# Last expert round taken out of the loop and added on TensorE, expert weights loaded in halves

## The reference, cut to what matters

```python
act = silu(xt @ exp_w1[e]) * (xt @ exp_w3[e]) * comb      # w1, w3: 1024 x 256 per expert
out = out + act @ exp_w2[e]                               # w2: 256 x 1024 per expert
y = rms_norm(x + out, final_norm_g)
```

## Time and profile before

| | |
|---|---|
| median of 3 runs | 716.58 us (715.87 to 720.83) |
| profiled execution, own time | 718.26 us |
| its span, first to last instruction | 716.3 us |
| mean granted TensorE clock | 0.931 |
| busy: TensorE, VectorE, ScalarE, POOL | 618.3, 319.0, 201.5, 79.2 us |
| moved by DMA | 179.38 MB, mean 250 GB/s |

### The profile page before, as it was taken

One profiled execution on the slowest core, in us unless ns is written; L12 is line 12 of the kernel. 1 busy time (PEld: TensorE's weight loads), 2 busy tenths in 40 slices (PEclk: granted clock), 3 DMA queues, 4 the chain that ended last, 5 costly groups with the idle time before them and its releaser, 6 DMA issues.

```text
span 716.3 us, 11504 instructions
## 1 busy us (share of the span) xinstructions
PE 618.3 (86%) x4673; PEld 451.2 (63%) x4673; DVE 319.0 (45%) x629; ACT 201.5 (28%) x343; POOL 79.2 (11%) x129
## 2 busy tenths in 40 slices
PE   4999999989899999999989985999999798398720
PEld 3999998579899999984778862333333343033200
DVE  4748978958544364688413155121121121012038
ACT  5512332254743434436003051121121121012022
POOL 0000000510001210010202111111212111110100
PEclk8999999999999999999989985999999999699965
DMA  9941220324556233669896394899999999999453
GB/s 284 279 141 64 96 82 2 121 79 125 168 129 214 81 118 119 234 239 342 277 389 254 150 350 181 337 420 420 418 421 421 418 422 419 422 420 402 190 233 136
DMA packets 74924, 179.38 MB, mean 250 GB/s; under 512 B 9166, under 2 KB 55946, under 8 KB 61544
## 3 DMA queue, kind: packets, MB, share of 16 engines
q1 hardware_dynamic: 65900, 163.47, 60.9%
q0 software_dynamic: 5600, 12.76, 4.7%
q10 hardware_dynamic: 3372, 2.42, 1.0%
HBM read 172.80 MB, written 15.61 MB: 263 GB/s over the span
## 4 chain that ended last, share of the span: by engine, by line
PE 68%; DMA 17%; DVE 6%; SPq 4%; issue 3%; ACT 2%; ACTq 1%; DVEq 0%; POOLq 0%
DMA w<-exp_w 13%; PE ps L1678 12%; PE ps L1680 12%; PE ps L1679 12%; PE ps L2121 11%; PE ps L2149 4%; PE ps L1827 3%; SPq L612 3%; PE ps L1674 3%; PE ps L1908 2%; DMA raw<-cache_mem_k 2%; DMA xs_rows<-x_sample 1%; PE ps L2008 1%; PE ps L1845 1%; PE ps L1970 1%
## 5 line engine op out<-in xcount | busy, mean ns | idle before, releaser
L2121 PE MATMUL ps<-w,xeT 128*64 128x512 f32 (+2 forms) x512 | 122.9, 652 | 22.9 <-DMA w<-exp_w 21.6
L1678 PE MATMUL ps<-xH,w_h 128*128 128x260 f32 x480 | 139.0, 290 | 0.4 <-DVE xL L1336 0.2
L1679 PE MATMUL ps<-xH,w_l 128*128 128x260 f32 x480 | 136.2, 284 | 0.0
L1680 PE MATMUL ps<-xL,w_h 128*128 128x260 f32 x480 | 136.2, 284 | 0.0
L2121 PEld LDWEIGHTS ps<-w,xeT 128*64 128x64 f32 (+2 forms) x512 | 42.2, 147 | 102.0 <-issue 100.2
L1678 PEld LDWEIGHTS ps<-xH,w_h 128*128 128x128 f32 x480 | 91.1, 190 | 5.6 <-issue 4.9
L1679 PEld LDWEIGHTS ps<-xH,w_l 128*128 128x128 f32 x480 | 91.0, 190 | 0.2
L1680 PEld LDWEIGHTS ps<-xL,w_h 128*128 128x128 f32 x480 | 91.1, 190 | 0.0
L1028 DVE TENSOR_TENSOR w_l<-raw,w_h 128x2048 fp32r<-128x2048 f32 x28 | 64.1, 2289 | 35.5 <-ACT w_h L725 35.5
L2149 PE MATMUL ps<-w,aT 128*64 128x512 f32 (+2 forms) x256 | 58.6, 598 | 9.3 <-DVE aT L1591 9.3
L1584 DVE SCALAR_TENSOR_TENSOR gated<-ps,rs_slot,silu 128x256 f32<-128x256 f32 x14 | 6.8, 483 | 122.3 <-ACT silu L966 122.3
(11 more groups left out here) (364 smaller groups left out, 920.2 us busy)
## 6 DMA issues: line engine op xcount, KB each, us to landing
w<-exp_w SPq DMA_DIRECT2D x96, 1024.0 KB, 21.7
raw<-w_in SPq DMA_DIRECT2D x8, 1024.0 KB, 11.1
raw<-cache_mem_k SPq DMA_DIRECT2D x8, 1024.0 KB, 6.8
raw<-cache_mem_v SPq DMA_DIRECT2D x8, 1024.0 KB, 12.1
raw<-xa_wk SPq DMA_DIRECT2D x4, 1024.0 KB, 5.9
raw<-xa_wv SPq DMA_DIRECT2D x4, 1024.0 KB, 5.7
raw<-xa_wq SPq DMA_DIRECT2D x4, 1024.0 KB, 5.1
raw<-xa_wo SPq DMA_DIRECT2D x4, 1024.0 KB, 5.2
```

Source lines behind the costliest of these rows:

```text
L1678: pe.matmul(out, h1, h2, start=start, stop=False)
L1679: pe.matmul(out, l1, h2, start=False, stop=False)
L1680: return pe.matmul(out, h1, l2, start=False, stop=stop)
L2121: last = pe.matmul(mm[0][half, j, :], xeT[j][:, k, half], w13[s][:, :, k, :], start=k == 0, stop=k == KT_D - 1)
```

## The change

It has these parts, all in one diff:

1. The last round (places 28 and 29, slots 2 and 3) stands behind the loop, and a turn of the loop is one round (places 30 and 31, slots 0 and 1, then those over capacity). The number of rounds is the same as before where the loop makes one turn. The gathers of the two are exchanged, so that the parity fits. The last round's transposes stand before the loop; the loop's turn ends with the transposes of a further gather, which is used only if there is another turn.
2. The last round's rows are not stored to `y_rows`. Instead TensorE adds them: per tile of tokens `x2` times the identity plus `ye[1]` times `back`, a 128 x 128 matrix that has the token's weight where row and token meet. VectorE's two adds come before it. ScalarE's squares and VectorE's last product read the sum from PSUM.
3. `back` is made in the routing, before `route_done`: the weights of the last round's rows by ten products of one column (`last_w`), and five fills.
4. Rows of `y_rows` that nobody stores to must be zero: VectorE fills `sumsq`, and SP writes it over `y_rows` by two transfers, after the eighth load of w_in.
5. `x2` is loaded by tiles, in the order of `TAIL`; `yr_in` counts both.
6. The gate and up weights are loaded in two halves of the contraction (4 KB per partition), with semaphores of their own; `hidden` waits for each half before its products, and counts `half_ready` after the fourth step, on which the next load of the first half waits.
7. Nine semaphores of the routing become two that count.

```diff
+TURNS = 1 + OVER // 2
+HALF = KT_D // 2 * FF
+TAIL = (0, 4, 1, 2, 3)
...
+        def in_whole(n_t):
+            return ps[(0, 2, 3, 1, 0)[n_t]][:].rearrange("p b d -> p (b d)")
...  (SP)
                 if c == 9:
+                    sp.wait_ge(zero_made, 1)
+                    zeros = sumsq[:, 0:SEQ].rearrange("p (o d) -> p o d", o=1)
+                    sp.dma_start(y_rows[0:8 * P].rearrange("(p a) (h d) -> p (a h) d", p=P, h=2),
+                                 zeros.broadcast_to([P, 16, SEQ])).then_inc(y_zeroed, 16)
+                    sp.dma_start(y_rows[8 * P:2 * T]...).then_inc(y_zeroed, 16)
...
+            def load_half(s, e, h):
+                dst = w13[s][:].rearrange("p w k f -> p w (k f)")
+                c = slice(h * HALF, h * HALF + HALF)
+                for n, src in enumerate((w1, w3)):
+                    sp.dma_start(dst[:, n:n + 1, c],
+                                 src[bass.ds(e, 1)].rearrange("o p f -> p o f")[:, :, c]).then_inc(w13_in[h][s], 16)
...
-                    sp.wait_ge(hid_ready, q + 1)
-                    for p, e in zip(coming, which):
-                        load_gate_up(p % RING, e)
+                    for h, free in enumerate((half_ready, hid_ready)):
+                        sp.wait_ge(free, q + 1)
+                        for p, e in zip(coming, which):
+                            load_half(p % RING, e, h)
...
             with sp.Fori(0, loops_n) as it:
-                for r in range(2):
-                    ...
+                which = [expert_at(it * 2 + (FIXED + 2 + n)) for n in range(2)]
+                ...
+            which = [expert_at(FIXED + n) for n in range(2)]
+            for h, free in enumerate((half_ready, hid_ready)):
+                sp.wait_ge(free, FREE_AT[1])
+                for n in range(2):
+                    load_half(2 + n, which[n], h)
+            sp.wait_ge(y_done, FREE_AT[1])
+            for n in range(2):
+                load_down(2 + n, which[n])
             sp.wait_ge(y_done, PAIRS)
-            sp.dma_start(x2[:, 0:4, :], x_rows[0:SEQ].rearrange("(t p) d -> p t d", p=P)).then_inc(x_back, 16)
-            sp.dma_start(x2[0:NS, 4, :], x_rows[SEQ:T]).then_inc(x_back, 16)
+            for t in TAIL:
+                t0, n = TILES[t]
+                sp.dma_start(x2[0:n, t, :], x_rows[t0:t0 + n]).then_inc(yr_in[t], 16)
...
-            for j in range(2):
-                wait(y_stored[j], loops_n * 16 + 16 * (PAIRS // 2))
+            wait(y_stored[0], loops_n * 16 + 16 * (PAIRS // 2))
+            sp.wait_ge(y_stored[1], 16 * (PAIRS // 2))
...  (ScalarE, before, in and after the loop)
+            columns_left(PAIRS + 1, 1)
             with act.Fori(0, loops_n) as it:
                 act.wait_ge(rs_made, it + 1)
+                silu_of(it + PAIRS, 0, rs_now[:, 0:1])
+                y_left(it + PAIRS, 0, it * 16 + 16 * (PAIRS // 2))
+                act.wait_ge(hid_ready, it + (PAIRS + 1))
+                columns_left(it + (PAIRS + 2), 0, False)
+            silu_of(loops_n + PAIRS, 1, rs_slot[:, PAIRS:PAIRS + 1])
+            y_left(loops_n + PAIRS, 1, 16 * (PAIRS // 2))
...  (VectorE, routing)
-            for i in range(1, OVER // 4):
+            for i in range(1, OVER // 2):
...
+            dve.scalar_tensor_tensor(last_hot[:], slot_f[:, 1], float(PAIRS), wgt[:], ALU.is_equal, ALU.mult).then_inc(last_hot_ready, 1)
+            link(dve.tensor_copy(row_f[:], gids[:, PAIRS:PAIRS + 1]))
+            dve.tensor_scalar(row_t[:], tile_no[:], row_f[:, 0:1], -1.0, ALU.subtract, ALU.mult)
+            src = take("last_w")
+            dve.tensor_copy(w_slot[:], src[:, 0:1]).then_inc(tv_used, 1)
+            dve.wait_ge(tv_used, TV_AT["last_w"] + 1)
+            for t in range(NT):
+                last = dve.tensor_scalar(back[:, t, :], count_to[:], row_t[:, t:t + 1], w_slot[:, 0:1], ALU.is_equal, ALU.mult)
+            last.then_inc(route_done, 1)
...  (VectorE, tail)
+            for n_t in range(2):
+                add_experts(TAIL[n_t])
+            dve.wait_ge(fg_in, 16)
+            for n_t in range(NT):
+                if n_t + 2 < NT:
+                    add_experts(TAIL[n_t + 2])
+                mean_square(n_t)
...  (TensorE, routing, behind rs_ids and before the first gathered_columns)
+            out = open_tv("last_w")
+            pe.wait_ge(last_hot_ready, 1)
+            for i in range(2):
+                for j, (_, n) in enumerate(TILES):
+                    last = pe.matmul(out[:, 0:1], row_hot[0:n, i, j, :], last_hot[0:n, i, j:j + 1], start=(i, j) == (0, 0),
+                                     stop=(i, j) == (1, NT - 1))
+            last.then_inc(tv_ready, 1)
...  (TensorE, hidden)
                 for k in range(KT_D):
+                    if k % (KT_D // 2) == 0:
+                        for s, count in loads:
+                            pe.wait_ge(w13_in[2 * k // KT_D][s], count * 32)
...
+                    if k == KT_D // 2 - 1:
+                        last.then_inc(half_ready, 1)
...  (TensorE, loop and behind it)
+            gathered_columns(PAIRS + 1, 1, PAIRS // 2 + 1)
             with pe.Fori(0, loops_n) as it:
+                ...
+                hidden(it + PAIRS, 0, slots, False)
+                act_columns(it + PAIRS)
+                down(it + PAIRS, slots)
+                gathered_columns(it + (PAIRS + 2), 0, it + (PAIRS // 2 + 2))
+            pe.wait_ge(xa_ready, loops_n + (PAIRS + 2))
+            pe.wait_ge(xv_ready, loops_n + (PAIRS + 2))
+            hidden(loops_n + PAIRS, 1, slots, False)
+            act_columns(loops_n + PAIRS)
+            down(loops_n + PAIRS, slots)
+            pe.wait_ge(ya_ready, loops_n + (PAIRS + 1))
+            pe.wait_ge(yv_ready, loops_n + (PAIRS + 1))
+            for n_t, t in enumerate(TAIL):
+                n = TILES[t][1]
+                pe.wait_ge(y_sum, n_t + 1)
+                if n_t == 4:
+                    pe.wait_ge(y_out, 1)
+                for b in range(2):
+                    c = slice(512 * b, 512 * b + 512)
+                    out = in_whole(n_t)[0:n, c]
+                    pe.matmul(out, ident[0:n, 0:n], x2[0:n, t, c], start=True, stop=False)
+                    last = pe.matmul(out, back[:, t, 0:n], ye[1][:, c], start=False, stop=True)
+                last.then_inc(whole, 1)
...  (POOL, loop)
+                wait(xt_done, it + (PAIRS + 2))
+                gather(0, g_idx[:, 0:1])
+                wait(y_stored[0], it * 16 + 16 * (PAIRS // 2))
+                ...
+                scatter(None, 0, s_idx[:, 0:1])
```

More of the change, by code:

```diff
@@ L65 @@
 OVER = 2 * T // CAP
-MORE_ITEMS = EXPERTS - FIXED + OVER
-COLS = PAIRS + MORE_ITEMS // 2 + 2
+TURNS = 1 + OVER // 2
+COLS = PAIRS + 2 + TURNS
 LIST = BAND
 assert COLS <= LIST
+HALF = KT_D // 2 * FF
 RING = 7
-TURNS = MORE_ITEMS // 4
+ROUTE_BY_PE = {"count": 1, "rank": 2, "block": 3, "starts": 4, "place": 5}
+ROUTE_BY_DVE = {"less": 1, "at_place": 2, "at_rank": 3, "over": 4}
 EXPERT_BYTES = 3 * SLOT_BYTES
@@ L461, in trunk_kernel @@
         out_stored = sem("out_stored")
-        w13_in = [sem(f"w13_in{i}") for i in range(RING)]
+        w13_in = [[sem(f"w13_in{i}_{h}") for i in range(RING)] for h in range(2)]
         w2_in = [sem(f"w2_in{i}") for i in range(RING)]
@@ L484, in trunk_kernel @@
         y_sum = sem("y_sum")
+        zero_made = sem("zero_made")
+        y_zeroed = sem("y_zeroed")
+        last_hot_ready = sem("last_hot_ready")
+        whole = sem("whole")
         y_sq = sem("y_sq")
@@ L487, in trunk_kernel @@
         y_root = sem("y_root")
-        y_out = [sem(f"y_out{i}") for i in range(NT)]
+        y_out = sem("y_out")
         y_saved = sem("y_saved")
         fg_in = sem("fg_in")
-        x_back = sem("x_back")
         route_done = sem("route_done")
@@ new lines, in _ @@
+                rounds = sp.value_load(free_at[0:1, bass.ds(it, 1)], min_val=1, max_val=PAIRS + TURNS)
+                for h, free in enumerate((half_ready, hid_ready)):
+                    wait(free, rounds)
+                    for n in range(2):
+                        load_half(n, which[n], h)
+                wait(y_done, rounds)
+                for n in range(2):
+                    load_down(n, which[n])
+            which = [expert_at(FIXED + n) for n in range(2)]
+            for h, free in enumerate((half_ready, hid_ready)):
+                sp.wait_ge(free, FREE_AT[1])
+                for n in range(2):
+                    load_half(2 + n, which[n], h)
```

216 lines of the change are left out of this document (96 added, 120 removed).

## The result

The changed kernel takes **723.91 us** (median of 7 runs, 722.2 to 726.01), the kernel before 717.62 beside it (7 runs, 714.93 to 720.83). The ratio is **1.0088, 95% interval 1.0068 to 1.0109**: certainly slower, by 6.3 us, just under what the prediction called 1% (7.2 us). The forecast was 716.9 with a range up to 722.

What follows compares the result with a forecast made beforehand. The expert part was taken as bound by an unbroken transfer queue from 458 us. Routing +7.7, early release -3.4, halves +0.5 made it 4.8 late; expert rows at 687.9 plus tail gave 716.65, adjusted to 716.9 us (range 708 to 722).

Steps and rivals of the forecast that it cites:

- The routing step: End of routing: new steps, including ten one-column calls at 4.3 us, start ScalarE's xeT of round 0 7.7 us late.
- The release of the first refill: Queue restart after round 0: halves release it 3.4 us earlier, so with routing 4.3 us later than before.
- The zeroing and VectorE's fill: Early, before TensorE's projections: expected free under cover; without it up to 10 us for zeroing and 0.64 for the fill.
- The tail from the first add: From 687.9 to 716.65 us: adds, sums, norm and store, with TensorE's first 5 us at the lower clock.
- the rival in which it stays low: Tail: TensorE stays at the lower clock, five tiles of 6.9 us, giving 730.6 us; chance 0.1.
- The last rounds: Rounds 14 and 15 on TensorE: start 656.4, last product ends 684.5, copies done 685.2 us.
- Halves, in the queue: Gate and up loads as 512 KB with 4 KB rows: 0.5 us taken from 0 to 3.7, queue 4.8 late.
- 4 KB rows pay 9 ns: Rival in the weight queue: a fixed cost per row adds 3.2 us, giving 720.1 us; chance 0.1.
- The early restart: Rival: queue restarts early, at -0.8 us lateness, giving 711.3 us, or 708.5 with the clock up; chance 0.17.
- the read-back ahead of the queue: Rival: expert rows are read without waiting behind the queue, tail starts at 685.2, giving 714.2 us; chance 0.15.
- a second turn: Rival: the loop makes two turns, adding 9.3 + 3.65 us and its transfers, about 730 us; chance 0.01.
- A fixed part of 0.22 for each transfer: Rival in the queue: a tenth of 2.2 us shows for each of 50 more transfers, 11 us, 727.9; chance 0.02.

Runs made afterwards that it cites:

- f_rows4k: Kernel before, each 1 MB gate and up load issued as two of 512 KB with 4 KB rows, released and awaited together; 724.26 us, ratio 1.0103.
- a_whole: Changed kernel with gate and up weights loaded whole again (1 MB, 8 KB rows); 723.70 us, ratio 1.0087.
- d_free_w: Changed kernel with the last round's weight column riding in the list of norm factors and the five fills after the first copies; 717.39 us, ratio 1.0004.
- e_waits: Changed kernel with TensorE's waits for ScalarE's copied columns moved behind products that don't read them; 726.90 us, ratio 1.0112.
- p_free_waits: Changed kernel, weight column in factor list, whole loads except halved first refill, copy waits behind products not needing them; 713.33 us, ratio 0.9933.
- j_both: Changed kernel with both the edits of d_free_w and e_waits, halves kept; 717.77 us, ratio 0.9995.
- c_mixed: Changed kernel with the upper half of the contraction loaded and multiplied first in every second slot; 728.57 us, ratio 1.0139.
- o_free_first: d_free_w with whole weight loads except the first refill, which is in halves; 715.49 us, ratio 0.9966.
- h_both_whole: j_both with whole gate and up weights in rows of 8 KB; 716.26 us, ratio 0.9973.

## Why the prediction was wrong

**Where the 7.0 us lie.** The forecast was 716.9, the median is 723.91. In the trace, the first add starts 5.2 later than forecast (693.13 instead of 687.9) and the tail behind it is 1.4 shorter (27.3 instead of 28.75): 3.8. The other 3.3 lie in the step from the trace to the median. The prediction carried over that the traced execution of before had taken 1.7 more than the median; the traced one of the changed kernel took 1.7 less than its median, and the median of before itself went up by 1.0 with more runs. The starts of xeT above show how much single executions differ; the prediction gave no reason why the difference should carry over.

**Right.** The routing step: 7.7 forecast for xeT, 7.4 measured (8.4 by ScalarE's idle time); the ten calls 4.3, measured 4.66. The release of the first refill: 4.3 forecast, 4.2 measured. The zeroing and VectorE's fill: no trace of a cost. The tail from the first add came out with the clock up, so the rival in which it stays low is refuted for this kernel. Its shape differs: no sums at the lower clock, where the prediction had 5 us of them.

**The steps that failed: "The last rounds", and with it the queue's end.** The prediction had the last product end at 684.5 and the first expert rows land at 687.9, so that the adds waited for the queue alone. Both came at 692.5, and the adds started at 693.13 behind the copies. The 8.0 us of the last rounds, by that step's own terms:

- Round 14 was to start at 656.4, on the assumption that all before it is at most 4.8 later. It started at 659.92, 3.5 more. Down(13) was 5.7 later than before, and the wait for ScalarE's copies of round 15's columns (1.80) was left out here, though the like wait ahead of round 15 was counted: the program makes it ahead of both.
- Each down product was put at 3.65 and took 5.35: 3.4 for two. The prediction carried over a duration from a round of before, and with it that round's clock.
- The turns between `hidden` and `down` were 2.5 and 2.6 instead of 2.1, and the transposes with copies 2.6 instead of 2.3: 1.2 together.

These make 8.1.

**The size that was off: "Halves, in the queue".** I took 0.5 of a range of 0 to 3.7 and gave the upper end a chance of 0.1. From the refill to the landing of the gains the changed kernel takes 4.9 more than the kernel before. By the rows it would be 4.4: 6,400 more of them at 11.0 ns on 16 engines. The fixed 9 ns a row that I had worked out from the 1 KB rows was nearly right, and I set it aside for one window of one microsecond, 4 KB rows of another matrix at 418 GB/s. What the queue does at 413 in the long run, and 398 in a stretch, that window could not show. The Trainium skill's rule ("DMA: Bandwidth & Descriptors", Bandwidth: at least 1 MiB for 75% of peak) points in the right direction and is far off in size: f_rows4k, with all gate and up loads at 512 KB, holds 412 where whole loads hold 420.

**Consequence.** The sum had routing on one side (+7.7) and the shorter tail with the early release on the other, and they were to cancel. By the traces the side of the gains brought 3.3 (271.3 to 268.0 after xeT); in a_whole, without halves, it is 1.4 (269.9), but the medians of the two are the same. The loss is of the size of the routing step, which I had priced rightly (d_free_w: without it 1.0004). I believed too much of the gain, because I took TensorE's last rounds from the old kernel and the rate of the halves from its best case. Each of the two mistakes alone would have put the first add at about the same time: the paths ended together, and in e_waits, where TensorE's chain was shortened, the queue made the adds wait until the same point (241.2 after xeT, 240.7 in the changed kernel).

**The rivals.** "4 KB rows pay 9 ns" gave 720.1 and was nearest, with the right mechanism for one of the two paths. The early restart, the read-back ahead of the queue and a second turn did not occur. A fixed part of 0.22 for each transfer would have been 11 us; the queue grew by 4.9, and the rows alone make 4.4.

## What to carry to other kernels

Where a queue that runs without a gap sets the time, the release won by splitting transfers must be held against the price of every shorter row behind it: here it was even (a_whole against the changed kernel), and with the rest of the loads whole it came out ahead (p_free_waits against j_both). A small value that is wanted late should ride in a product that is made anyway: ten one-column calls and what had to come before them put the first round 7.4 us later, more than the new tail won (5.3). When a wait for data goes away, walk the engine's own program for the stretch behind it, with every wait it makes for another engine, and don't carry durations over from rounds in which its clock was different. Two paths that end together hide each other: shortening one of them shows nothing until the other is shorter too. And one traced execution is no median: take the step between them as uncertain by as much as executions scatter.

## Not expected of the hardware

- Loads of the same bytes with each row cut in two, in twice as many transfers: 412 to 414 GB/s in 500 to 580 instead of 420 at the same busy share, 11 ns for each row more. Between 580 and 620 us it is 393 to 398, in all seven kernels that have every gate and up load in halves, and 420 in the six others; why the stretch is slow was not found.
- Loads into 64 partitions instead of 128: 251 GB/s in a mix with whole loads, an estimated 209 for themselves, busy share 1.02, and 162 us for the kernel.
- TensorE's clock at the start of the tail differs between kernels with the same instructions there. The first pair of sums took 1.10 after 3.40 of idle time (changed, a_whole, c_mixed, o_free_first), and 2.04 to 2.05 after 4.38, 4.95, 5.02, 6.85 and 7.04 (d_free_w, h_both_whole, p_free_waits, j_both, e_waits): some 2 us of what was won before the tail are lost again. The idle time may not be the whole reason: in the four kernels of the first group the last down products had run partly at 1.2 GHz (5.18 to 5.35) and the clock was up again before the tail; in the second group only those of e_waits had. Which of the two decides was not tested.
